# One hybrid decoder layer on one core: norm after the projection, other order of chunks, a wide meta block, other places for late loads and gathered dots

## What is computed

```python
h = concatenate([meta(16), x(512), pad])                  # float32, 1024 wide
xn = rms_norm(h, mix_norm_gain)
aq, ak, av, bq, bk, bv, iq, ik, iw, gate_a, gate_b = split(xn @ w_in)
# differential attention: 4 heads, two softmaxes each, head norms and rope on aq, ak
p1 = masked_softmax(q1 @ k1 * scale); p2 = masked_softmax(q2 @ k2 * scale)
a_out = rms_norm((p1 - lam * p2) @ v, a_subln_gain) * 0.8
# sparse attention: 8 index heads choose 128 keys for each query
index_score = sum_h iw * relu(iq @ ik);  valid = top_k(index_score, 128)
b_out = softmax(bq @ bk over valid) @ bv                  # 8 heads, one shared key and value
h = h + (sigmoid(gate_a) * (a_out @ w_branch_a) + sigmoid(gate_b) * (b_out @ w_branch_b)) @ w_out
# product-key experts: 8 heads choose 16 of 128 x 128 experts for each token
hn = rms_norm(h, ffn_norm_gain)
expert, top_s = top-16 of the pair sums of two top-16s of (hn @ w_query) . sub_keys
act = gelu(u[expert] . hn)
h = h + sum over the 8 x 16 chosen of softmax(top_s) * act * v[expert]
return h[16:528]
```

## Time and profile before

| | us |
|---|---|
| three runs | 1858.65, 1867.12, 1867.56 |
| their median | 1867.12 |
| the profiled execution | 1865.89 |
| its span | 1864.1 |
| PE busy (matmuls) | 1771.8 (95% of the span) |
| DVE busy | 1343.9 (72%) |
| ACT busy | 721.1 (39%) |
| POOL busy | 664.0 (36%) |
| granted TensorE clock, mean | 0.974 of full speed |
| bytes moved | 429.78 MB, 231 GB/s over the span |

### The profile page before, as it was taken

How to read it: one execution, slowest core, us unless ns; L and a number is a source line. 1 busy time by engine, 2 the same in 40 slices (tenths; PEclk the granted TensorE clock), 3 DMA queues, 4 the chain that set the end, 5 groups by cost and what they waited for, 6 DMA issues and landing times.

```text
span 1864.1 us, 24836 instructions
## 1 busy us (share of the span) xinstructions
PE 1771.8 (95%) x8767; PEld 1478.1 (79%) x8767; DVE 1343.9 (72%) x2706; ACT 721.1 (39%) x1201; POOL 664.0 (36%) x416
## 2 busy tenths in 40 slices
PE   5899998999888999999989999999899999999998
PEld 4788885555555679999989998999788888888886
DVE  6843268555655869979979943991688888888885
ACT  4323334232223233455435632653343334433442
POOL 3223320000000333677586777775322222222220
PEclk9999997999889999999999999999999999999999
DMA  3222213434243663588888899986999999999993
GB/s 127 68 71 92 92 40 113 136 136 133 93 141 131 211 199 114 164 308 283 283 328 259 286 370 417 303 282 194 387 361 329 338 325 334 334 326 339 323 333 117
DMA packets 170192, 429.78 MB, mean 231 GB/s; under 512 B 15328, under 2 KB 66144, under 8 KB 165744
## 3 DMA queue, kind: packets, MB, share of 16 engines
q1 hardware_dynamic: 133056, 294.23, 46.2%
q0 software_dynamic: 36864, 134.23, 19.5%
q10 hardware_dynamic: 176, 0.07, 0.0%
HBM read 384.44 MB, written 44.04 MB: 230 GB/s over the span
## 4 chain that ended last, share of the span: by engine, by line
PE 74%; DVE 5%; DMA 3%; ACT 1%; POOL 1%; issue 1%; DVEq 0%; ACTq 0%
PE psum L1869 29%; PE psum L1161 9%; PE psum L1162 8%; PE psum L1163 8%; PE psum L1103 6%; PE psum L1187 5%; PE psum L1090 3%; PE psum L1011 3%; DMA u<-in_u 2%; PE psum L1059 1%; POOL ul L1401 1%; DMA act_mat<-act_w 1%; PE psum L1142 1%; PE psum L1037 1%; DVE score L1432 1%
## 5 line engine op out<-in xcount | busy, mean ns | idle before, releaser
L1401 POOL TENSOR_TENSOR ul<-u,uh 128x1024 fp32r<-128x1024 f32 x128 | 324.4, 2536 | 513.2 <-ACT uh L1319 512.0
L1161 PE MATMUL psum<-split,uh 128*128 128x384 f32 x1024 | 356.3, 348 | 13.0 <-POOL ul L1401 13.0
L1163 PE MATMUL psum<-split,ul 128*128 128x384 f32 x1024 | 344.3, 336 | 0.0
L1162 PE MATMUL psum<-split,uh 128*128 128x384 f32 x1024 | 344.2, 336 | 0.0
L1849 POOL DMA_INDIRECT v_row<-in_v,gv x128 | 122.6, 958 | 382.2 <-DVE psum L1927 368.6
L1869 PE MATMUL psum<-vl,wh 128*128 128x512 f32 x768 | 240.5, 394 | 0.0
L1161 PEld LDWEIGHTS psum<-split,uh 128*128 128x128 f32 x1024 | 194.0, 189 | 18.0 <-POOL ul L1401 16.2
L1162 PEld LDWEIGHTS psum<-split,uh 128*128 128x128 f32 x1024 | 193.9, 189 | 1.4 <-issue 1.4
L1163 PEld LDWEIGHTS psum<-split,ul 128*128 128x128 f32 x1024 | 193.4, 189 | 0.0
L1869 PEld LDWEIGHTS psum<-vl,wh 128*128 128x128 f32 x768 | 144.6, 188 | 33.8
L1927 DVE SCALAR_TENSOR_TENSOR psum<-v_row,w,psum 128x1024 f32<-128x1024 f32 x127 | 162.9, 1283 | 0.0
(11 more groups left out here) (291 smaller groups left out, 3368.7 us busy)
## 6 DMA issues: line engine op xcount, KB each, us to landing
u<-in_u SPq DMA_DIRECT2D x128, 512.0 KB
v<-in_v SPq DMA_DIRECT2D x64, 1024.0 KB
act_mat<-act_w SPq DMA_DIRECT2D x128, 192.0 KB
act_v<-act_mat SPq DMA_DIRECT2D x64, 384.0 KB
wraw<-in_w_wide SPq DMA_DIRECT2D x18, 1024.0 KB, 5.3
gate_mat<-stage SPq DMA_DIRECT2D x16, 1024.0 KB
gate<-gate_mat SPq DMA_DIRECT2D x128, 128.0 KB
w_low<-in_w_branch_b SPq DMA_DIRECT2D x8, 1024.0 KB, 5.2
```

The source lines that it names most:

```text
L1161: nc.tensor.matmul(out, high[:, c], split[:, 0:DENSE, 0, c], start=(c == 0), stop=False)
L1162: nc.tensor.matmul(out, high[:, c], split[:, 0:DENSE, 1, c], start=False, stop=False)
L1163: last = nc.tensor.matmul(out, low[:, c], split[:, 0:DENSE, 0, c], start=False, stop=(c == DC - 1))
L1401: nc.gpsimd.tensor_tensor(ul[:, n % U_COLS], u[:, n % U_COLS], uh[:, n % UH_COLS].bitcast(F32), ALU.subtract).then_inc(s["u_low"], 1)
```

## The change

It has these parts.

1. *Norm.* The tiles of x are transposed as loaded (`turn_x`), times the norm gain and split. The squares (`squares_of`) are taken by ACT between the high parts, the inverse norm `inv_x` is made after the last low part, and it multiplies the results: as a scale of ACT's evacuation, and on DVE as one more operation of `head_scale` and in `iw`. The first piece of weights is split in two halves on ACT and POOL, PE waits for the second half only at the third row chunk, and the loads are issued as x0, piece 0, x1, x2, piece 1, x3. POOL's clearing of `akT`, `bkT`, `ikT` moves behind the first piece, with two new ones for the meta tile of `av` and `bv`.
2. *Chunks.* "av" now stands ahead of "small".
3. *Meta block.* The first 128 columns of the probabilities are turned and multiplied by a value tile that is zero below its 16 meta rows; for i < 3 one ACT copy takes all blocks. For i = 3 PE turns the meta block behind `beside`, and ACT runs `beside` ahead of the exponentials and copies the meta block behind them.
4. *Dots.* All 32 groups of each turn have a dot (96 in place of 84), the gap has 14 in place of 28, the tail 10 in place of 8.
5. *Late stages.* `load_early` is split in two and issued at columns 116 and 120 in place of 124. The first high part of a gate (`high_of_w(act, 0)`) and the Gelu of the dots move ahead of the last pair of columns on ACT. The last column's sums are counted by tile (`tile_summed`), and each of the three last additions waits for its own tile.

The name of the change also speaks of "searches in parts". The routines of the searches (`search`, `find`, `best`, `chosen`, `chosen_beside`) and their table of steps are in no line of the diff.

```diff
-CHUNKS = ["ak", "small", "av", "aq", "gate", "iq", "gate", "bq", "gate", "gate"]
+CHUNKS = ["ak", "av", "small", "aq", "gate", "iq", "gate", "bq", "gate", "gate"]
...
             for i in range(NT):
                 sp.dma_start(m.stream[:, i, :], d.x[i * P:(i + 1) * P, :]).then_inc(x_loaded[i], 16)
-            load_weights(0)
-            load_weights(1)
+                if i in (0, 2):
+                    load_weights(i // 2)
...
-            nc.gpsimd.memset(m.akT[:], 0.0)
-            nc.gpsimd.memset(m.bkT[:], 0.0)
-            nc.gpsimd.memset(m.ikT[:], 0.0).then_inc(keys_zeroed, 1)
             for n in range(N_PIECES):
+                if n == 1:
+                    nc.gpsimd.memset(m.akT[:], 0.0)
+                    nc.gpsimd.memset(m.bkT[:], 0.0)
+                    nc.gpsimd.memset(m.av[:, NT], 0.0)
+                    nc.gpsimd.memset(m.bv[:, NT], 0.0)
+                    nc.gpsimd.memset(m.ikT[:], 0.0).then_inc(keys_zeroed, 1)
                 w = width_of(n)
-                pool.wait_ge(w_high, n + 1)
...
+                for k, chunks in enumerate(HALVES if n == 0 else (slice(0, PK),)):
+                    pool.wait_ge(w_high, parts_before(n) + k + 1)
...
-            normed(0)
-            normed(1)
+
             dve.wait_ge(mix_loaded, 16)
             for i in range(NT + 1):
...
                 nc.vector.tensor_tensor(scratch_of(i), ps, bcast(m.mix_gain[:], 2, r), ALU.mult).then_inc(gained_x, 1)
-                if i + 2 <= NT:
-                    normed(i + 2)
                 dve.wait_ge(gained_x, i + 1)
                 low_of(i)
 
+            dve.wait_ge(squared, NT + 1)
+            nc.vector.tensor_scalar(ms_x[:, 0:NT + 1], sums[:, 0:NT + 1], 1.0 / D, EPS, ALU.mult, ALU.add).then_inc(ms_ready, 1)
+            dve.wait_ge(root_ready, 1)
+            inverse_root(nc, step, inv_x[:, 0:NT + 1], root_x[:, 0:NT + 1], ms_x[:, 0:NT + 1])
+            nc.vector.tensor_copy(ms_x[:, 0:NT + 1], inv_x[:, 0:NT + 1]).then_inc(x_inverse, 1)
...
+                if heads == GROUPS:
+                    step(nc.vector.tensor_scalar(inv[0:r, 0:heads], inv[0:r, 0:heads], inv_x[0:r, i:i + 1], None, ALU.mult))
...
-                    nc.scalar.copy(m.av[0:r, i], ps).then_inc(evacuated, 1)
+                    nc.scalar.mul(m.av[0:r, i], ps, inv_x[0:r, i:i + 1]).then_inc(evacuated, 1)
...
-                pe.wait_ge(xn_ready, i + 1)
+                pe.wait_ge(x_loaded[i], 16)
...
-GAP_DOTS = 28
+GAP_DOTS = 14
...
-        plan += [("turn", i, g, 2 * TURNS_AT[i] + g // 2) for g in range(TURNS * TURN_GROUPS) if g % 8 != 7]
+        plan += [("turn", i, g, 2 * TURNS_AT[i] + g // 2) for g in range(TURNS * TURN_GROUPS)]
...
-                if n == N_KEYS - U_COLS:
-                    late.load_early(sp)
+                if n == 2 * TAIL_AT + 2:
+                    late.load_first(sp)
+                if n == 2 * TAIL_AT + 6:
+                    late.load_second(sp)
...
-                if (NT - 1) * UNITS + 2 <= step < NT * UNITS + 2:
-                    turn_last_meta(*ALL_UNITS[step - 2][1:])
                 if step < len(ALL_UNITS):
                     for key in scores_beside(*ALL_UNITS[step]):
                         score_of(*key)
                 beside(step)
+                if (NT - 1) * UNITS + 2 <= step < NT * UNITS + 2:
+                    turn_last_meta(*ALL_UNITS[step - 2][1:])
...
                 if early:
                     turn_out(*ALL_UNITS[step - 2])
+                if early:
+                    beside(step)
                 if step < len(ALL_UNITS):
                     for key in scores_of_unit(*ALL_UNITS[step]):
                         use_score(*key)
-                beside(step)
-                if 2 <= step and not early and step < len(ALL_UNITS) + 2:
+                if not early:
+                    beside(step)
+                if early:
+                    last_meta_out(*ALL_UNITS[step - 2][1:])
+                elif 2 <= step < len(ALL_UNITS) + 2:
                     turn_out(*ALL_UNITS[step - 2])
...
-            alone(PAIRS - 1, PAIRS)
+            late.high_of_w(act, 0)
             act.wait_ge(s["dotted"], PICKS)
             nc.scalar.activation(dots[:], dots[:], ACT.Gelu).then_inc(s["act0_ready"], 1)
+            alone(PAIRS - 1, PAIRS)
             late.high_parts(act)
...
-                mm.then_inc(s["summed"], 1)
+                    if last and k == RING - 1:
+                        mm.then_inc(s["tile_summed"], 1)
+                if not last or k < RING - 1:
+                    mm.then_inc(s["summed"], 1)
...
-        dve.wait_ge(s["summed"], N_KEYS)
         for i in range(DENSE):
+            dve.wait_ge(s["tile_summed"], i + 1)
```

151 lines of the change are left out of this document (85 added, 66 removed).

## The result

The changed kernel takes 1848.75 us (median of four runs, 1841.31 to 1850.26) beside 1866.9 before: the ratio is 0.9905, with a 95% interval of 0.9883 to 0.9928. It is 18 us faster; the prediction was 1824, 42 us faster, with 1810 to 1839 as its range. The time fell, but by less than half of what was forecast, and by more than the 0.5% that can be told from no change.

A forecast was written before the change was run, and what follows sets the result against it. PE was taken to bound the kernel, with 74% of the chain. Gains 9.2 + 11.7 + 6 + 5.1 + 7.5 + 2.3 = 41.8 us off 1865.9 gave 1824 us, range 1810 to 1839 for 8 in 10.

The forecast's parts named there:

- Head, 9.2: Head of the projection: first product at about 12.2 us, second piece of weights at 33.5 instead of 42.73; gain 9.2 us.
- rival A: Projection: POOL holds DVE at head and rotations; gains 5 and 7, not 9.2 and 11.7; 1833 us, chance 0.18.
- Chunks, 11.7: Projection: av slots ahead of small give DVE time for rotations, removing PE's waits and slow clock; gain 11.7 us.
- The meta block: First three query blocks: one ACT copy replaces two, PE's column counts stay the same; gain nothing.
- The late order, 6: Last query block: ACT's side copies ahead of its exponentials remove most of PE's waits for copies; gain 6 us.
- Rival B: Mixers give nothing: DVE ends the wait in ACT's place, or PE's clock falls elsewhere; 1830 us, chance 0.15.
- rival C: Last query block: without waits PE stays at 2.4 GHz, 6 us more, and a full head; 1815 us, chance 0.15.
- Dots, 5.1: Gap and turns: halving the gap's dots gains 7 us, dots moved to the turns cost 1.9; net 5.1.
- Rival D: Turns become DMA-bound as late rows add to PE's time, making the kernel slower; chance 0.02.
- Between the products, 7.5: Between the expert products: earlier loads and gate high part cut PE's 6.76 us wait to 1.2; gain 7.5 us.
- End, 2.3: Kernel's end: two of three last additions run beside the last tiles' products; gain 2.3 us.
- Rival E: Searches don't change as named; if other parts overlapped poorly, time within 0.5%, about 1860 us; chance 0.03.

The follow-up runs named there:

- e2: Changed kernel with POOL's memsets moved behind the low part of the second piece of weights: 1845.52 us, ratio 0.99 to before.
- e4: Changed kernel with three rows of v gathered ahead in place of six before and eight after the first expert product's end: 1843.49 us, ratio 0.9891.
- e7: Changed kernel with the last query block's old order (meta block turned and copied at once, `beside` behind the exponentials): 1837.62 us, ratio 0.9856.
- e1: Kernel before with only the chunk order changed, av ahead of small: 1864.37 us, ratio 1.0002.
- e15: e13 with the old chunk order, small ahead of av: 1821.52 us, ratio 0.9764.
- e3: Changed kernel with POOL's low parts of the weights in four operations, one per row chunk: 1844.58 us, ratio 0.9897.
- e14: Kernel before with the 128-wide meta block, old mixer order, and `high_of_w(act, 0)` ahead of the dots' Gelu: 1855.21 us, ratio 0.9944.
- e12: Changed kernel with the last query block's meta block turned and copied at once, `beside` still ahead of the exponentials: 1831.7 us, ratio 0.9834.
- e13: Changed kernel with the edits of e2, e3, e4 and e12 together: 1820.35 us, ratio 0.9754.
- e11: Changed kernel with the edits of e2, e3, e4 and e7 together: 1828.07 us, ratio 0.9805.
- e9: Changed kernel with the dots as before: 28 in the gap, none in every eighth group of a turn: 1853.2 us, ratio 0.9945.

## Why the prediction was wrong

The sign and the dots were right; the size was off by more than half, and by these steps of the sum. The largest is the order of the chunks, 11.7 us for nothing. The 5.7 us of the first three query blocks, which the prediction put at nothing, hide a part of the shortfall; that is luck.

**Head, 9.2: mis-sized, and rival A held in part.** The first product came at 13.78, not 12.2: ACT loads a table (1.28 us) ahead of its first cast, an item of no row in the sum, and DVE's first low part took 1.52. The larger part is the order on POOL. I wrote that the memsets "now stand between the pieces and are done ten us before they matter". They matter at once: they push the second piece's low part from 17.54 us, where e2 has it, to 21.87, and there it meets the third tile. Measured at slot 5: 3.6 with the hold, 8.4 without (e4, e7), 10.2 with the memsets later (e2).

**Chunks, 11.7: wrong.** "With the ten av slots between, DVE has two wide slots for each rotation" took the earlier trace rows for a matter of DVE's time alone. Two things bind there that don't depend on the order: slots 13 and 14 wait for a PSUM bank in which a rotation still works, and the rotations of small have to be paid at some later place. There three of POOL's low parts hold DVE for 4.4 us or more, as three did before, at the old place; the prediction counted one hold at the head and one in the tables, and none of these. But they aren't what ate the gain: e1 puts the step at zero with them and e15 without them. In the first 98 us it looked as forecast; a gain read in one stage must be followed to where the next stage starts.

The rule of the Trainium skill ("SBUF — State Buffer", "SBUF: two separate sides") was cited in the prediction for low parts of x, where it decided. The rows agree that the hold lasts for POOL's whole instruction: DVE's row ends 1.09 us, about its own length, behind POOL's (27.49 and 26.40), and with POOL's work in four operations the long rows are gone (e3). They also show that whoever starts first isn't held and the other is (in e4 DVE's 1.23 us at 21.83, POOL's 5.57 at 21.91), and that operations with one input tile can be held (the copy of 4.55 us at 123.11).

**The meta block, "Nothing" for three query blocks: wrong, by 5.7.** "PE's transposes and products have the same column counts" was true and not enough: a product over 16 rows costs 0.12 to 0.14 us more than one over 128 (e14).

**The late order, 6: wrong.** The waits named were the right ones, and with the meta block handled at once they go (e12), for 8 to 9.5 us (e13 beside e11), though DVE's out_b then keeps PE for 4.3. The step never priced what was moved with them: PE's turn of the meta block behind `beside`, and ACT's copy behind the exponentials, where ACT waits up to 7.57 us for PE. Together they gave nothing in that block and 1.4 less behind it; the price of the late meta block alone is some 14 us between e12 and the changed kernel by the ratios. What is queued behind a moved instruction, and who waits for it, was asked of the copies and not of the turn. Rival B has both its causes in the traces, DVE in ACT's place and falls of the clock elsewhere; rival C, a last block without falls, came only with e12's order.

**Dots, 5.1: right in kind, a little small.** Gap 9.3 by the profiles for my 7, turns 1.7 for my 1.9; by time 6 to 7.5 (e9). Rival D, DMA-bound turns, is out: DVE's period with a dot is still 2.99 us.

**Between the products, 7.5: right where I looked, given back behind it.** PE's wait fell from 6.76 to 0.82. "SP's gates for the second pair go out 5 us sooner as well, so the loads keep up" was the failing half: they go out sooner, but beside ten of POOL's gathers of `v`, and land only after 10 us, against 5 with three gathers ahead (e4).

**End, 2.3: right**, 2.4 measured: the second span ends 4.3 us behind its last product in place of 6.8.

Rival E is half true: no search differs, and nothing of the result needed it.

## What to carry to other kernels

Follow a gain to the next stage that starts late or early, with a table of starts from both timelines; a wait that leaves one window and stands in the next is no gain. When an order is changed by hand, price every instruction that moves, the small one that another engine stands still for above all; here the late copy of 16 keys' probabilities cost more than the side copies gained. Give a POOL operation that runs beside DVE short pieces, and gathers that run beside loads a short queue.

## What the runs showed that was not expected

Among products over 128 rows, one over 16 rows was dearer with the same columns: 0.12 to 0.14 us each at 2.4 GHz. DVE's low part of x and POOL's of the weights exclude each other by who starts first (4.83 for 1.23 us, or 5.57 for 4.53), so that 0.8 us at 20 us move the rest of the kernel by 5, from one execution to the next; memsets of POOL didn't hold DVE (1.23 us in e2). And falls of the clock to 1.2 GHz, two of them behind waits of 2.2 and 2.0 us, made the same 555 products 8.4 us longer in one kernel than in another.
